# Splitting the first expert's weights inside the output projection, and turning the first further chunk behind the first expert

## What is computed

```python
def _hier_moe(x, w_group, b_group, w_expert, b_expert, w1, w3, w2):
    ...
    g_p, g_idx = lax.top_k(g_prob, 1)
    ...
    e_p, e_idx = lax.top_k(jax.nn.softmax(e_sel, axis=-1), MOE_TOPK)
    gate_w = g_p * e_p / jnp.sum(e_p, axis=-1, keepdims=True)
    ...
    hidden = jax.nn.silu(jnp.einsum('nd,edf->nef', xt, w1)) * jnp.einsum('nd,edf->nef', xt, w3)
    y = jnp.einsum('nef,efd->nd', hidden * combine[:, :, None].astype(hidden.dtype), w2)
    return y.reshape(b, t, d)

def _block(x, mod, mixer, ln, moe):
    sh1, sc1, g1, sh2, sc2, g2 = jnp.split(mod[:, None, :], 6, axis=-1)
    y, extras = mixer(x * (1.0 + sc1) + sh1)
    x = _layer_norm(DEEPNORM_ALPHA * x + g1 * y, ln[0], ln[1])
    x = _layer_norm(DEEPNORM_ALPHA * x + g2 * _hier_moe(x * (1.0 + sc2) + sh2, *moe), ln[2], ln[3])
    return x, extras
```

## Time and profile before

| | |
|---|---|
| median of 3 runs | 1848.85 us (1846.56 to 1856.86) |
| profiled execution, its own time | 1855.64 us |
| its span | 1853.8 us |
| TensorE matmul / weight load busy | 1459.9 us (79%) / 1151.2 us |
| VectorE / ScalarE / GpSimd busy | 967.6 / 639.4 / 453.3 us |
| mean granted TensorE clock | 0.894 |

### The profile page before, as it was taken

One profiled execution on the slowest core, in us unless ns is written; L12 is line 12 of the kernel. 1 busy time (PEld: TensorE's weight loads), 2 busy tenths in 40 slices (PEclk: granted clock), 3 DMA queues, 4 the chain that ended last, 5 costly groups with the idle time before them and its releaser, 6 DMA issues. The chain is left out here.

```text
span 1853.8 us, 23467 instructions
## 1 busy us (share of the span) xinstructions
PE 1459.9 (79%) x8491; PEld 1151.2 (62%) x8492; DVE 967.6 (52%) x1530; ACT 639.4 (34%) x1016; POOL 453.3 (24%) x210
## 2 busy tenths in 40 slices
PE   4799999656999998188993199989997862988870
PEld 1688888555577445166772199987884442766750
DVE  0412122276377252645775835418994755646558
ACT  1311212242344111155773412115552121746543
POOL 1000000112000032335775500010000232645556
PEclk8899999877899999589997599999998885999995
DMA  8576754701000810357995032220005322867863
GB/s 273 177 238 210 245 183 160 173 12 31 1 1 1 278 76 24 136 206 279 387 388 203 23 94 69 70 62 10 1 1 173 136 97 84 326 255 289 310 222 142
DMA packets 125055, 280.10 MB, mean 151 GB/s; under 512 B 12441, under 2 KB 64369, under 8 KB 112657
## 3 DMA queue, kind: packets, MB, share of 16 engines
q1 hardware_dynamic: 113984, 239.15, 37.3%
q0 software_dynamic: 10096, 36.33, 5.7%
q10 hardware_dynamic: 864, 3.15, 0.4%
HBM read 248.99 MB, written 34.85 MB: 153 GB/s over the span
## 5 line engine op out<-in xcount | busy, mean ns | idle before, releaser
L489 PEld LDWEIGHTS psum<-exact 128*128 128x128 f32 x3360 | 411.0, 191 | 57.8 <-issue 57.8
L489 PE MATMUL psum<-exact 128*128 128x258 f32 (+1 forms) x3360 | 421.0, 286 | 23.9 <-PEq L331 23.9
L1925 PE MATMUL psum<-exact,exact 128*128 128x512 f32 x912 | 222.3, 399 | 1.4 <-issue 0.9
L1925 PEld LDWEIGHTS psum<-exact,exact 128*128 128x128 f32 x912 | 171.9, 191 | 46.6 <-issue 8.7
L807 PE MATMUL psum<-higher 128*128 128x512 f32 x400 | 174.0, 595 | 2.7 <-PEq L733 2.7
L575 DVE COPY lower<-psum 128x258 f32<-128x258 f32 (+1 forms) x70 | 29.7, 424 | 239.6 <-PE psum L489 239.6
L807 PEld LDWEIGHTS psum<-higher 128*128 128x128 f32 x400 | 75.8, 191 | 95.5 <-issue 94.0
L2077 DVE TENSOR_TENSOR exact<-higher,exact 128x2048 fp32r<-128x2048 f32 x40 | 107.3, 2681 | 48.1 <-ACT exact L2022 48.1
L1299 ACT ACTIVATE higher<-psum,higher 128x640 f32<-128x640 f32 (+1 forms) x120 | 84.3, 706 | 119.7 <-DVE higher L1245 119.7
L533 ACT COPY lower<-psum 128x258 f32<-128x258 f32 (+1 forms) x70 | 26.1, 373 | 287.3 <-PE psum L489 287.3
L1202 PE MATMUL psum<-higher 128*128 128x320 f32 (+1 forms) x384 | 116.3, 440 | 5.0 <-PEq L1392 1.7
(11 more groups left out here) (307 smaller groups left out, 2392.3 us busy)
## 6 DMA issues: line engine op xcount, KB each, us to landing
higher<-in_moe_w SPq DMA_DIRECT2D x50, 1024.0 KB, 8.4
higher<-in_ada_w SPq DMA_DIRECT2D x48, 1024.0 KB, 5.2
lower<-in_moe_w SPq DMA_DIRECT2D x46, 1024.0 KB, 8.1
y_rows<-higher SPq DMA_DIRECT2D x32, 512.0 KB, 4.8
higher<-in_ev_w_in SPq DMA_DIRECT2D x15, 1032.0 KB, 7.7
higher<-in_od_w_in SPq DMA_DIRECT2D x11, 1024.0 KB, 5.2
lower<-mod_rows SPq DMA_DIRECT2D x16, 512.0 KB, 8.9
higher<-in_ev_w_out SPq DMA_DIRECT2D x4, 1536.0 KB, 12.2
```

The source lines that it names most:

```text
L489: last = T.matmul(bank(g % W_BANKS)[:, 0:cw], a, b[:, k], start=(k == 0 and m == 0), stop=(k == KD - 1 and m == 2))
L1925: last = T.matmul(bank(2), a[:, k, :], w, start=(k == 0 and m == 0), stop=(k == KD - 1 and m == 2))
```

## The change

1. The rounding and subtraction of expert 0's two up halves move from `router` into `mix_out`: ScalarE rounds a half behind the normalisation of tile 2 and of tile 3, GpSimd subtracts behind `norm.late` of the same tile.
2. The subtraction for its down weight moves from GpSimd in `router` to VectorE at the start of `experts`. `router` has no GpSimd work left.
3. The first further chunk is transposed and split behind expert 0's down-projection, on all three engines, and no longer before the loop.
4. Buffers move to make room; the load of expert 1's down weight goes from `mix_out` to `router`, and `pool.drain()` is added at the end of retention.

```diff
@@ layout
+        LOW2_AT = [BIG + 12 * D + W13, BIG + 8 * D, BIG + 10 * D]
+        HIGH13_AT = [(BIG + 12 * D + W13 + W2, R + 17 * D), (BIG, BIG + W13 // 2), (BIG + W13, BIG + W13 + W13 // 2)]
+        HIGH2_AT = [R + 2 * W13 + n * W2 for n in range(2)]
@@ mix_out, sync
                     load2(sp, 0, I["moe_w2"][i, 0])
-                    load2(sp, 1, I["moe_w2"][i, 1])
@@ mix_out, scalar
                             norm.normalise(act, t)
+                        if t in (2, 3):
+                            act.wait_ge(up_in[0][t - 2], 16)
+                            A.copy(high13(0, t - 2), raw13(0, t - 2)).then_inc(high_w, 1)
@@ mix_out, gpsimd
                         pchain.step(norm.late(pool, nc.gpsimd, pchain, t))
+                        if t in (2, 3):
+                            pool.wait_ge(high_w, t - 1)
+                            nc.gpsimd.tensor_tensor(low13(0, t - 2), raw13(0, t - 2), whole(high13(0, t - 2)), ALU.subtract).then_inc(low_w, 1)
@@ retention, gpsimd
                         nc.gpsimd.tensor_tensor(g, g, cens[:, t % 2], ALU.mult).then_inc(gated, 1)
+                    pool.drain()
@@ router, sync
                     load13(sp, 1, I["moe_w13"][i, 1])
+                    load2(sp, 1, I["moe_w2"][i, 1])
@@ router, gpsimd
-                    for h in range(2):
-                        pool.wait_ge(high_w, h + 1)
-                        nc.gpsimd.tensor_tensor(low13(0, h), raw13(0, h), whole(high13(0, h)), ALU.subtract).then_inc(low_w, 1)
-                    pool.wait_ge(high_w2, 1)
-                    nc.gpsimd.tensor_tensor(low2(0), raw2(0), whole(high2(0)), ALU.subtract).then_inc(low_w2, 1)
-                    pool.drain()
@@ router, scalar
-                    act.wait_ge(up_in[0][0], 16)
-                    A.copy(high13(0, 0), raw13(0, 0)).then_inc(high_w, 1)
                     act.wait_ge(nm, 1)
...
-                    act.wait_ge(up_in[0][1], 16)
-                    A.copy(high13(0, 1), raw13(0, 1)).then_inc(high_w, 1)
@@ experts, tensor
                         down(4, s, b, lambda: pe.wait_ge(h_low, e + 1), y_s)
+                        if isinstance(e, int) and e == 0:
+                            pe.wait_ge(o_in, 16)
+                            turn_half(xg_o, 0, bank(3), o_turned)
+                            pe.wait_ge(o_xl, 1)
+                            turn_half(xg_o, 1, bank(3), o_turned)
@@ experts, scalar (and alike in experts, vector)
                         A.copy(yb[:, b, 0:BANK], bank(4)).then_inc(y_a, 1)
+                        if isinstance(e, int) and e == 0:
+                            x_of_further(0, 0)
+                            x_of_further(0, 1)
...
                     x_of(0)
-                    x_of_further(0, 0)
-                    x_of_further(0, 1)
@@ experts, vector
                     dve.nop().then_inc(o_yd, 1)
+                    dve.wait_ge(high_w2, 1)
+                    V.tensor_tensor(low2(0), raw2(0), whole(high2(0)), ALU.subtract).then_inc(low_w2, 1)
```

37 lines of the change are left out of this document (15 added, 22 removed).

## The result

| | before | changed |
|---|---|---|
| median, us | 1851.1 (5 runs, 1846.56 to 1856.86) | 1836.14 (5 runs, 1829.79 to 1837.98) |
| ratio, 95% interval | | 0.9905 [0.9882, 0.9928] |
| second comparison (23 and 6 runs): medians, then the ratio and its 95% interval | 1855.5 | 1833.62: 0.9876 [0.9853, 0.9900] |
| profiled execution, its span | 1855.64, 1853.8 | 1829.79, 1827.9 |

The change made the kernel faster by 0.95% in the first comparison and 1.24% in the second: 13 to 22 us and 19 to 27 us. The prediction was 1823 us in a range of 1810 to 1831. The sign was right; the time lies above the range in both comparisons.

A forecast was written before the change was run, and what follows sets the result against it. Routing was taken as bound by VectorE's chain, held up by GpSimd's subtractions. 25.1 + 3.0 - 2.4 - 0 = 25.7 us off 1855.64 gave 1829.9, or 1823 us from the median 1848.85; range 1810 to 1831.

The forecast's parts named there:

- Term 1: Routing without GpSimd: three held VectorE instructions become short, 12.55 us gained in each layer, 25.1 in all.
- Term 2: The moved roundings and subtractions between the projection's tiles: just fit, cost 0, up to 0.4 us.
- Term 3: Drain at the end of retention: latent attention starts 2.4 us later, counted once; bounds 0 and 2.4.
- Term 4: Start of the experts: first up-projection at 783.7, not 793.32, including +1.3 us for a held indirect DMA (bounds 0 and 2.3).
- rival C: Start of the experts: a subtraction does not hold an indirect DMA; 3.3 us gained a layer, 1819.5 us; chance 0.06.
- Term 5: Further chunk behind expert 0: collision, idle TensorE and lower clock leave expert 1 1.5 us earlier a layer, 3.0 in all.
- rival A: Behind expert 0, VectorE's second long subtraction starts before GpSimd's and ends on time; 6.5 us gained a layer, 1813 us; chance 0.25.
- B: Routing does not shorten, its three long VectorE instructions having another reason; 1848 us; chance 0.04.
- D: Expert loop locks into a bad phase, 28 experts each waiting up to 2.9 us; slower, 1904 us; chance 0.03.

The follow-up runs named there:

- experiment 4: Changed kernel with GpSimd's three subtractions of expert 0's weights put back into routing; 1855.45 us, 1.0004 of the kernel before.
- experiment 9: Changed kernel with GpSimd's drain replaced by a late wait of ScalarE and VectorE in latent attention's first block; 1832.41 us, 0.9879 of the kernel before.
- experiment 5: Changed kernel with the subtraction for expert 0's down weight given from VectorE to GpSimd, between its first two gathers; 1830.27 us, 0.9865 of the kernel before.
- experiment 1: The changed kernel run and profiled again, nothing altered; 1833.62 us, 0.9876 of the kernel before.
- experiment 6: Changed kernel with GpSimd's subtraction for expert 1 moved ahead of its fourth gather, in expert 0 only; 1826.27 us, 0.9841 of the kernel before.
- experiment 2: Changed kernel with the further chunk turned ahead of the expert loop again, as before the change; 1834.79 us, 0.9883 of the kernel before.
- experiment 8: Changed kernel with the edits of experiment 5, experiment 6 and experiment 7 together, and a late wait instead of the drain; 1816.88 us, 0.9776 of the kernel before.
- experiment 10: Changed kernel with GpSimd's further-chunk gather moved ahead of its subtraction for the next expert's down weight, in every expert; 1822.48 us, 0.9822 of the kernel before.
- experiment 7: Changed kernel with the further chunk turned inside expert 0 rather than behind it; 1823.09 us, 0.9822 of the kernel before.

## Why the prediction was wrong, point by point

**The start of the count.** Against the second comparison this is the largest part. The sum was made against the profiled execution (1855.64, so 1829.9) and then carried over to the median of three runs, 1848.85, which made it 1823. 45 further executions of the kernel before, in three sets, have medians of 1855.5, 1856.1 and 1855.3: the median of three lay 6.6 us low, and the profiled execution was the typical one. The sentence that failed is "taken from that, 1823 us"; the 4 us that were added to the range for the spread did not cover it. With 1855.5 and the 22.5 us of the table, one gets 1833, and the second comparison gave 1833.62. The first comparison does not divide in the same way: its own base was 1851.1 and its medians differ by 15.0 us only, so of the 13.1 us between 1823 and 1836.14 the base makes 2.3 there and the smaller difference 10.7. Its interval of 13 to 22 us just reaches the 22 of the stages.

**Term 1, routing, 25.1 us.** Right: 12.57 and 12.55, from 12.55. Experiment 4 shows the mechanism, not only the size. The sixth load is one fifth more than five, not one sixth; the measured share makes it 0.72 x 21.35 = 15.4 us of DMA work, near the 16 that were taken.

**Term 2, the projection, 0.** Right in size, but it does not "just pass". GpSimd's subtraction of tile 3 in the second layer takes 4.98 us, not 4.5, and VectorE's L895 (now L900) of the last tile starts 0.26 us before its end:

```profile
1486.31 4.98 POOL L866 TENSOR_TENSOR exact<-lower,exact 128x2048 fp32r<-128x2048 f32 x1
```

```profile
1491.03 0.81 DVE L900 SCALAR_TENSOR_TENSOR lower<-lower 128x512 f32<-128x512 f32 x1
```

It takes 0.81 us, not 0.69. In the first layer the same line is held to 3.73 and 3.72 us under the two subtractions, and the wait behind it takes that up. From the last tile's first instruction on VectorE (L892, now L897) to the router it takes 14.13 us, 14.02 before, in the second layer and 23.97, 24.10 before, in the first.

**Term 3, the drain, -2.4.** Right mechanism; 2.0 and 2.5 in the two profiles, 2.8 by the two groups of experiment 9. The bound "0, if something catches up" is out.

**Term 4, expert 0 earlier.** Its first product was put at 783.7 - 774.3 = 9.4 us after the first copy and stands at 9.4 and 9.2. The held indirect DMA was put at +1.3: it took 2.31 against 1.05, +1.26 (experiment 5 shows that it goes with VectorE's subtraction). Here the Trainium skill, SBUF — State Buffer, section SBUF: two separate sides, would have had the issue unhindered, as the prediction reads it; the runs show otherwise (2.31 us against 1.05), so rival C falls. Expert 0 itself was taken at its old length and took 8.47 us for its first products, not 7.80, 0.7 us missed. Over the first layer's profiles this group takes 7.5 (experiment 5) to 8.6 us (experiments 1 and 6), and 8.2 in experiment 2, where the further chunk's transposes come ahead of it as before; what sets it within these bounds stays open.

**Term 5, the further chunk, +3.0.** The step that failed among the terms: with the start's delays in it, the experts were put 3.0 us shorter in the two layers together, and they are as long as before (223.7 and 248.0 in the mean of three profiles, 223.7 and 247.8 before). Its events are right one by one (the collision, 4.45 us, the idle stretch of about 4 us, the lower clock), and rival A, which needed VectorE first, did not come. Two sizes were missing. The stretch of 1.85 us ahead of expert 1, which the control instructions of the branch and the loop explain, was put at nothing. And the cold up-projection costs 8.31 - 5.73 = 2.6, not 2.05. With the 0.7 us of expert 0 these make 3.1 us. By the prediction's sum expert 1 starts 27.9 to 28.9 us after the first copy (802.2 to 803.2, less 774.3); it stood at 30.2. Its further chunk stood 0.9 us later than before; in the second layer expert 2, which follows there, stood 1.3 later; I had 1.5 gained. The forecast also stopped there, with the argument that behind expert 0 "TensorE is the busy engine, so what is gained before it stays gained". That sentence is wrong: TensorE waits in the further chunks for GpSimd's gathers (experiments 2, 8, 10), and experiment 7 gets back only part of its early gain for the same reason.

Four kernels, taken together, show which half of the edit costs and which gains. Experts, us, first and second layer:

| | VectorE's subtraction not there | VectorE's subtraction first |
|---|---|---|
| chunk turned ahead of the loop | 223.7, 247.8 (before) | 227.7, 250.6 (experiment 2) |
| chunk turned behind expert 0 | 219.5, 245.7 (experiment 4) | 223.7, 248.0 (changed, mean of three) |

Turned behind expert 0, the chunk gains 4.0 to 4.2 us in the first layer and 2.1 to 2.6 in the second; VectorE's subtraction costs 4.0 to 4.2 and 2.3 to 2.8, where the prediction's price for it was 1.3. So the zero is the sum of two effects, and the price of the subtraction was the one that was mis-sized. At expert 1 the subtraction's price is still as predicted (30.2 against 29.0, 29.8 against 28.5). The rest arises later; in the first layer 1.4 to 3.2 us of it lie between the first product of the second further chunk and that of the expert behind it, which take 12.5 us in experiment 4 and 13.9, 15.7 and 15.7 in the three profiles of the changed order, with waits for rows of 1.6 to 2.0 us and first down products of 2.09 us in the one and over 3 in the others. The lower row and experiment 2 have the rest of the edit in them, and the kernel before has not. With that, and with one profile in most cells, how much of this is the subtraction's doing and how much varies by itself stays open; the second layer's differences lie within its spread of 3 us.

**Rivals.** B and C fall as above. D, the loop locked into a bad phase, did not come: neither profile of the changed kernel shows TensorE waiting for VectorE's weight subtraction in each expert. A did not come; experiment 6 shows what it would have given in this place: 3.9 us a layer, not the 6.5 that it was priced at. The stretch of "issue" stays (2.36 us), and the clock fell too (7.35 us for 5.75), where A had it that so short a wait should not cost the clock.

**Left open.** What makes untouched stages differ by up to 3.5 us between executions of the same code was not tried. In the second layer three profiles of the same order give 249.9, 247.1 and 246.9; nearly all of that difference arises in the last further chunk, in which TensorE waits 2.65 us for rows in the first of them and 1.40 and 1.49 in the others, and whose first down products take 3.58 us in the first and 2.09 in experiment 1. Why the rows come late in one execution was not looked for.

## What to carry to other kernels

Take GpSimd's long elementwise instructions away from beside a chain of short VectorE ones: here each of three subtractions of 4.5 us stretched one instruction of 0.18 us to more than 4. When one edit moves two things, price them apart: here one gained what the other cost. Before counting an early start as gained, follow it to the next place where the fast engine waits for another; here that was a gather queued behind a subtraction that nobody needed yet, and exchanging the two was worth as much as the earlier start of experiment 7 (10 us each). And take the base of a forecast from many executions, or from none: state the difference, and let the range carry the spread of a median of three.
